# A two-block transformer forward pass: one factor per token for two norms in a row, and state-space decays by an fp32r product with a two-hot selector

## The chip, the cores and the metric

The kernel runs on one core of a Trainium2 chip. The metric is the device time of one execution in microseconds, lower is better. A core has TensorE (PE, products into PSUM), VectorE (DVE), ScalarE (ACT), GpSimd (POOL) and SyncE (SP, which issues DMA); each runs its own instructions in order, and they wait for each other on semaphores.

## The reference, cut to what matters

Two blocks run one after the other on 256 tokens of width 1024. The first has a hybrid mixer (a state-space mixer and gated linear attention), a cross-attention on 256 memory tokens and a SwiGLU feed-forward net, and ends with a norm. The second puts 16 meta tokens ahead, and has a stick-breaking attention, a squared-ReLU MLP, an RG-LRU mixer, a second MLP and a norm. The places that the change touches:

```python
def rmsnorm(x, g):                                 # rms_norm of the second block is the same
    return x * lax.rsqrt(jnp.mean(x * x, axis=-1, keepdims=True) + EPS) * g

# state-space mixer, per chunk of 64 tokens
a_cs = jnp.cumsum(a, axis=-1)                      # a = dt * A, 16 heads
Lmat = segsum_exp(a)                               # exp(a_cs[l] - a_cs[s]) for s <= l, else 0
y_diag = jnp.einsum('bcgls,bgrcls,bcsgrp->bclgrp', CB, Lmat, X)
...
# end of the first block, start of the second
h = h + swiglu(rmsnorm(h, norm_ffn[i]), w_ffn_in[i], w_ffn_out[i])
x = rmsnorm(h, norm_final)
...
h = jnp.concatenate([meta, x], axis=1)             # 16 + 256 tokens
hn = rms_norm(h, norm_mix[0])
h = h + stick_breaking_mixer(hn, sb_w_qkv[0], sb_w_o[0])
```

So the 256 real tokens pass two norms in a row at the border, with nothing between them; the 16 meta tokens pass the second alone.

## The kernel before

**Layout.** Activations lie transposed: feature on the 128 partitions, 8 blocks (KB) of features, tokens along the free dimension (T1 = 256, T2 = 272 with the meta tokens). The residual stream is hT. Weights come as a stream of 368 units of 128x1024 fp32 (`raw`, a ring of 4 buffers). For each unit ScalarE makes `whi`, the value rounded to fp32r (`split_hi`, L964), and VectorE makes `wlo`, the rest (`split_lo`, L1389). An operand is split likewise into `xh` (ScalarE, `operand`) and `xl` (VectorE, `operand_lo`, L1396). A product is then three fp32r products: xh·whi, xl·whi, xh·wlo (`products`, L420 to L422). A unit of TensorE is 8 feature blocks x 3 products into one of four `acc` banks, and `unit_done`, `lo_ready` and `evacuated` tie the engines together. The splits are made four units ahead.

**Norms.** The gain of a norm is multiplied into the operand before the product; the factor 1/rms of each token is applied to the product's result when VectorE moves it out of PSUM. The sum of squares comes from ScalarE's `square` of each block, VectorE's running sum over blocks (`add_stream_squares`, L1417), and an fp32 product with a matrix of 1/1024 (`stream_stats`, L481), which also spreads it over all partitions. `rms` (L982) takes the root on ScalarE, `inverse_rms` (L1430) the reciprocal on VectorE. For tokens on the partitions, products of one column give the same as columns (L485), and `rtok` holds the reciprocals.

**The border.** After the last of the 22 units of the FFN's second product (`ffo`), the statistics `fin1` are made, VectorE's `final` multiplies all eight blocks of hT by gain and factor (L1778), ScalarE and VectorE make xh, xl and squares of the result for the attention (norm `sb`), and TensorE's first unit of queries and keys waits for these block by block; the statistics `sb` follow behind that unit.

**The attention.** Queries and keys of a pair of heads (two units) alternate with scores and softmax-like terms of the pairs before (`sb_scores`, `soft_abs`, `soft_terms`, `soft_sum`, `soft_hi`, `soft_lo`, `sb_after`): the tiles sp, softp, softh, softl and wT. Then values (`token_pair`), scores of the last 16 queries (`tail_scores`) and the outputs.

**The decays.** `csn` holds the running sums of 16 heads on 16 partitions. `decay_row` of a head spreads its row over all 128 partitions: the stationary operand is one column of the identity, repeated 128 times, the product is in fp32 (L549), and two bf16 products (L550, L551) add a large number where the mask is zero. ScalarE takes the exponential, GpSimd multiplies with CB, and `ssd_out` reads the result two units later. Two rows come behind every second unit from the 28th to the 42nd.

The order of the work is written out by hand in each engine's program; no planner sets it.

## Time and profile before

| what | before |
|---|---|
| median of 3 runs | 1277.48 us (1276.99 to 1279.16) |
| profiled execution | 1278.51 us, span 1276.8 us |
| mean granted clock of TensorE | 0.985 |
| TensorE busy | 1218.4 us, 95% |
| VectorE, ScalarE, GpSimd busy | 67%, 52%, 3% |

A profile shows one execution. "Idle before" stands in square brackets behind an instruction with the engine and instruction that ended the idleness. An fp32 product is recorded as two instructions (x2), an fp32r product as one. Starts of matmuls are the better guide: their ends overlap the next one. The granted clock is a share of the full 2.4 GHz.

### The profile page before, as it was taken

The page shows a single profiled execution, that of the slowest core. Times are in us where ns is not written, and L with a number is a line of the kernel's source. Part 1 is how long each engine was busy: PE and PEld are TensorE (multiplying, and loading weights), DVE is VectorE, ACT ScalarE, POOL GpSimd, SP SyncE. Part 2 cuts the span into 40 slices and gives each one's busy share as a digit, 9 for nine tenths or more (in the row PEclk, how much of TensorE's full clock was granted, in tenths as well). Part 3 has the DMA queues.
Part 4 walks back from the last instruction along what each step waited for, and adds up shares of the span by engine and source line. Part 5 has one row for each costly group of instructions (what it writes and reads, how often), then busy time and mean ns, then how long its engine had stood idle before and what let it go on. Part 6 is the DMA issues. An engine that isn't in the chain of part 4 may idle for free.

```text
span 1276.8 us, 25597 instructions
## 1 busy us (share of the span) xinstructions
PE 1218.4 (95%) x9661; PEld 1179.2 (92%) x9661; DVE 860.8 (67%) x1295; ACT 666.1 (52%) x999; POOL 40.1 (3%) x59
## 2 busy tenths in 40 slices
PE   5989999999999999999799999999999888999996
PEld 5989879999999999999788899999999888999996
DVE  5897665798756777765676536666455969766443
ACT  6443435756534666654546325656344685666431
POOL 1001220200000000000100000000000000000000
PEclk9999999999999999999899999999999989999999
DMA  5455333466653566566433205555565435565661
GB/s 198 131 169 167 109 100 116 133 219 185 177 163 131 150 189 190 181 186 189 137 115 117 100 34 165 168 177 170 177 177 171 147 100 177 180 187 181 184 184 61
DMA packets 56761, 197.54 MB, mean 155 GB/s; under 512 B 7136, under 2 KB 9440, under 8 KB 56560
## 3 DMA queue, kind: packets, MB, share of 16 engines
q1 hardware_dynamic: 54144, 194.01, 49.4%
q10 hardware_dynamic: 2544, 2.51, 0.6%
q8 instruction: 52, 0.85, 0.3%
q14 instruction: 21, 0.17, 0.0%
HBM read 195.45 MB, written 1.05 MB: 154 GB/s over the span
## 4 chain that ended last, share of the span: by engine, by line
PE 80%; DVE 13%; ACT 4%; issue 2%; DMA 1%; SPq 0%; DVEq 0%; ACTq 0%
PE acc L420 22%; PE acc L422 22%; PE acc L421 22%; DVE wlo L1389 4%; PE acc L465 2%; PE acc L466 2%; PE acc L467 2%; ACT whi L964 2%; PE mix L549 1%; DVE xc L1593 1%; DVE uu L1921 1%; DMA raw<-w 1%; PE mix L711 1%; PE mix L692 1%; PE mix L791 1%
## 5 line engine op out<-in xcount | busy, mean ns | idle before, releaser
L964 ACT ACTIVATE whi<-raw 128x1024 fp32r<-128x1024 f32 x368 | 387.8, 1057 | 433.6 <-PE acc L422 373.8
L1389 DVE TENSOR_TENSOR wlo<-raw,whi 128x1024 fp32r<-128x1024 f32 x368 | 449.2, 1223 | 217.0 <-ACT whi L964 216.7
L420 PE MATMUL acc<-xh,whi 128*128 128x256 f32 (+1 forms) x1664 | 478.3, 287 | 25.0 <-DVE xl L1396 21.6
L421 PE MATMUL acc<-xl,whi 128*128 128x256 f32 (+1 forms) x1664 | 474.8, 285 | 0.0
L422 PE MATMUL acc<-xh,wlo 128*128 128x256 f32 (+1 forms) x1664 | 474.2, 285 | 0.0
L420 PEld LDWEIGHTS acc<-xh,whi 128*128 128x128 f32 x1664 | 317.2, 191 | 30.9 <-DVE wlo L1389 17.9
L422 PEld LDWEIGHTS acc<-xh,wlo 128*128 128x128 f32 x1664 | 317.6, 191 | 0.0
L421 PEld LDWEIGHTS acc<-xl,whi 128*128 128x128 f32 x1664 | 316.0, 190 | 0.2
L421 PE MATMUL acc<-hl,whi 128*128 128x256 f32 (+1 forms) x688 | 195.5, 284 | 0.0
L420 PE MATMUL acc<-hh,whi 128*128 128x256 f32 (+1 forms) x688 | 195.0, 283 | 0.0
L422 PE MATMUL acc<-hh,wlo 128*128 128x256 f32 (+1 forms) x688 | 194.7, 283 | 0.0
L422 PEld LDWEIGHTS acc<-hh,wlo 128*128 128x128 f32 x688 | 129.9, 189 | 0.0
L421 PEld LDWEIGHTS acc<-hl,whi 128*128 128x128 f32 x688 | 129.4, 188 | 0.0
L420 PEld LDWEIGHTS acc<-hh,whi 128*128 128x128 f32 x688 | 129.1, 188 | 0.0
L420 PE MATMUL acc<-yh,whi 128*128 128x256 f32 (+1 forms) x320 | 91.1, 285 | 6.8 <-DVE yl L1994 3.9
L422 PE MATMUL acc<-yh,wlo 128*128 128x256 f32 (+1 forms) x320 | 90.5, 283 | 0.0
L421 PE MATMUL acc<-yl,whi 128*128 128x256 f32 (+1 forms) x320 | 90.4, 283 | 0.0
L420 PEld LDWEIGHTS acc<-yh,whi 128*128 128x128 f32 x320 | 60.4, 189 | 8.2 <-DVE wlo L1389 5.1
L422 PEld LDWEIGHTS acc<-yh,wlo 128*128 128x128 f32 x320 | 60.5, 189 | 0.0
L421 PEld LDWEIGHTS acc<-yl,whi 128*128 128x128 f32 x320 | 60.1, 188 | 0.0
L465 PE MATMUL acc<-whi,xh 128*128 128x256 f32 (+1 forms) x160 | 47.0, 294 | 2.8 <-DVE wlo L1389 2.8
L1871 DVE SCALAR_TENSOR_TENSOR t<-acc,rstd 128x272 f32<-128x272 f32 (+1 forms) x64 | 27.7, 432 | 31.3 <-PE acc L422 30.9
(327 smaller groups left out, 1440.7 us busy)
## 6 DMA issues: line engine op xcount, KB each, us to landing
raw<-w SPq DMA_DIRECT2D x368, 512.0 KB, 3.6
hT<-xT ACTq DMA_DIRECT2D x1, 1024.0 KB, 10.5
mem<-memT ACTq DMA_DIRECT2D x1, 1024.0 KB, 5.8
out<-hT SPq DMA_DIRECT2D x8, 128.0 KB, 2.0
xdt<-wsmall ACTq DMA_DIRECT2D x1, 192.0 KB, 10.6
pr<-par ACTq DMA_DIRECT2D x1, 114.0 KB, 10.2
hT<-metaT ACTq DMA_DIRECT2D x1, 64.0 KB, 12.4
bcn<-wa ACTq DMA_DIRECT2D x1, 32.0 KB, 10.2
```

What stands on the lines that cost most here:

```text
L420: nc.tensor.matmul(dst, whi[:, slot, n, :], rh, start=first, stop=False)
L421: nc.tensor.matmul(dst, whi[:, slot, n, :], rl, start=False, stop=False)
L422: return nc.tensor.matmul(dst, wlo[:, slot, n, :], rh, start=False, stop=last)
L465: nc.tensor.matmul(dst, ah[:, k, at:at + n], whi[:, s:s + 2, k, :], start=k == 0, stop=False)
L466: nc.tensor.matmul(dst, ah[:, k, at:at + n], wlo[:, s:s + 2, k, :], start=False, stop=False)
L467: last = nc.tensor.matmul(dst, al[:, k, at:at + n], whi[:, s:s + 2, k, :], start=False, stop=k == KB - 1)
L549: nc.tensor.matmul(dst[:, 0:384], sel, csn[:, :], start=True, stop=False)
L692: last = nc.tensor.matmul(mix[:, h % 2, 256 * t:256 * t + 256], xqT[:, 2 * h + i, P * t:P * t + P], xkT[:, 2 * h + i, :], start=i == 0, st ...
L711: last = nc.tensor.matmul(mix[:, xbank[h], 256 * vb:256 * vb + 256], xv[:, mt, c:c + P], probT[:, h, mt, :], start=mt == 0, stop=mt == 1)
L964: act.activation(whi[:, j, :, :].rearrange("p k c -> p (k c)"), raw[:, j, :], ACT.Copy)\
L1389: dve.tensor_tensor(wlo[:, j, :, :].rearrange("p k c -> p (k c)"), raw[:, j, :], whi[:, j, :, :].rearrange("p k c -> p (k c)").bitcast(F32 ...
L1871: dve.scalar_tensor_tensor(out=t4[:, j, 0:T], in0=acc[:, j, 0:T], scalar=0.0, in1=rstd[:, 0:T], op0=ALU.max, op1=ALU.mult).then_inc(evacua ...
```

## The change

**The decays.** The running sums are stored in `cs2`, a tile of fp32r over 128 partitions that is zero except for two copies: rows 0 to 15 hold the rounded value, rows 32 to 47 the rest. The stationary operand `sel2` has a one at row h and at row 32 + h. One fp32r product then spreads high and low part together.

**The border.** The two norms are taken as one. With r1 the factor of the first norm and s the mean square of its unscaled output (hT times the gain of `fin1`), the factor of the real tokens is 1/sqrt(s + EPS * (mean square of hT + EPS)), and the gain is the product of both gains (`both`). So the operands of the attention come straight from hT. They are made during `ffo`, as each block of the FFN's output is finished, with their squares in a tile `sqb`. The meta tokens' part is made at the start of `ffo`. The first unit of queries starts behind `ffo`; then come two statistics products, of `sb` and of `fin1`, the latter in its own bank. The factors of tokens on partitions are made by products of one column out of `rstd` (`token_scales`). The stream itself still needs the first norm: its reciprocal and the multiplications of hT (`stream_rms`, `stream_normed`) now stand in the values part of the attention.

```diff
         "st_gla0", "st_gla1", "st_mem", "st_xattn", "pt0", "pt1", "pt2", "pt3",
-        "st_ffn", "st_fin1", "st_sb", "st_mlp0", "st_lru", "st_mlp1", "st_fin2"]
+        "st_ffn", "st_sb", "st_fin1", "tok_sb", "st_mlp0", "st_lru", "st_mlp1", "st_fin2"]
 R = {name: n for n, name in enumerate(MISC)}
...
+BANK["st_fin1"], FREE["st_fin1"] = 2, R["st_sb"]
 OPER = {name: n for n, name in enumerate(["mix", "xattn", "ffn", "sb", "mlp0", "lru", "mlp1"])}
-STAT = {name: n for n, name in enumerate(["mix", "xattn", "ffn", "fin1", "sb", "mlp0", "lru", "mlp1", "fin2"])}
-
-
-SUMS = {name: KB - 2 if name in ("fin1", "fin2") else KB - 1 for name in STAT}
+STAT = {name: n for n, name in enumerate(["mix", "xattn", "ffn", "fin1", "mlp0", "lru", "mlp1", "fin2"])}
+
+
+SUMS = {name: KB - 2 if name == "fin2" else KB - 1 for name in STAT}
 SUM0 = {name: sum(SUMS[x] for x in list(STAT)[:n]) for name, n in STAT.items()}
...
         csn = sb("csn", [16, 384], stack=s1)
+        cs2 = sb("cs2", [P, 384], F32R, stack=s1)
+        sel2 = sb("sel2", [P, SSD_HEADS], F32R, stack=s1)
         ctok = sb("ctok", [P, 4, 16], stack=s1)
...
             pool.memset(one16[0:16, :], 1.0).then_inc(consts, 1)
-            pool.wait_ge(consts, 9)
+            pool.memset(khk[:, 0, 0:384], 0.0).then_inc(consts, 1)
+            pool.wait_ge(consts, 10)
+            pool.tensor_copy(cs2[:, :], khk[:, 0, 0:384]).then_inc(consts, 1)
...
                 dst = mix[:, h % 2, :]
-                sel = ident[0:16, h:h + 1].broadcast_to([16, P])
-                nc.tensor.matmul(dst[:, 0:384], sel, csn[:, :], start=True, stop=False)
+                sel = sel2[:, h:h + 1].broadcast_to([P, P])
+                if h == 0:
+                    pe.wait_ge(sums_lo, 2)
+                nc.tensor.matmul(dst[:, 0:384], sel, cs2[:, :], start=True, stop=False)
                 nc.tensor.matmul(dst[:, 0:P], identb[:, :], bigm[:, :], start=False, stop=False)
...
-            stream_stats("fin1", T1)
             HB = SSD_HEADS + XH
                 for i in range(2):
+                    if m + i == 0:
+                        pe.wait_ge(metal_ready, 1)
                     unit("sqk", 2 * m + i, (2 * m + i) % 4, xh, xl, T2, ready=operand("sb") if m + i == 0 else None)
                     if m + i == 0:
-                        stream_stats("sb", T2, tiles2)
+                        pe.wait_ge(sumb_ready, KB)
+                        mean_squares("st_sb", [sqb[:, KB - 1, :]], T2)
+                        stream_stats("fin1", T1)
+                if m == 1:
+                    token_scales()
+
+            def token_scales():
+
+                dst = misc_bank("tok_sb")
+                pe.wait_ge(rstd_ready, 5)
+                for t, (at, n) in enumerate(tiles2):
+                    last = nc.tensor.matmul(dst[0:n, t:t + 1], rstd[:, at:at + n], ident[:, 0:1], start=t == 0, stop=True,
+                                            skip_group_check=True)
+                last.then_inc(misc_ready, 1)
...
                 if p == 1:
-                    pe.wait_ge(misc_free, R["st_sb"] + 1)
+                    pe.wait_ge(misc_free, R["tok_sb"] + 1)
                 if p >= 2:
...
                         act.activation(sg1[:, c % 4, :], xc[:, c, :], ACT.Tanh).then_inc(conv_th, 1)
+                    if m == 5:
+                        act.wait_ge(dt_step, 5)
+                        act.activation(cs2[0:16, :], csn[:, :], ACT.Copy).then_inc(sums_hi, 1)
                     if m == 6:
...
                 split_hi(u0 + n + 4)
+                if n == 0:
+                    act.wait_ge(unit_done, u0)
+                    act.wait_ge(meta_ready, 1)
+                    act.activation(xh[:, :, 0:META], mtok[:, :, :], ACT.Copy).then_inc(metah_ready, 1)
+                    act.wait_ge(meta_in, 16)
+                    act.activation(sqb[:, :, 0:META], hT[:, :, 0:META], ACT.Square).then_inc(metasq_ready, 1)
                 if (FFN_KB * m + FFN_KB - 1) // 8 == n:
                     act.wait_ge(evacuated[m % 4], (OUTS["ffo"] + m) // 4 + 1)
+                    h = hT[:, m, META:T2]
+                    act.activation(xh[:, m, META:T2], h, ACT.Copy, scale=both[:, m:m + 1]).then_inc(xh_ready, 1)
+                    act.activation(sqb[:, m, META:T2], h, ACT.Square, scale=g("fin1", m)).then_inc(sqb_ready, 1)
                     square(m, T1)
                     m += 1
-            rms("fin1", T1, (), 4)
-            act.wait_ge(meta_in, 16)
-            for b in range(KB):
-                act.wait_ge(fin_step, b + 1)
-                operand("sb", b, T2)
-            rms("sb", T2, (P, P, META), 5)
+            act.wait_ge(misc_ready, R["st_sb"] + 1)
+            act.wait_ge(rstd_ready, 4)
+            act.activation(rt[:, 0:META], mix[:, MISCB, 0:META], ACT.Sqrt, bias=EPS)
+            act.activation(rt[:, META:T2], mix[:, MISCB, META:T2], ACT.Sqrt, bias=EPS * EPS).then_inc(misc_free, 1)
+            act.wait_ge(misc_ready, R["st_fin1"] + 1)
+            act.activation(rtf[:, :], mix[:, BANK["st_fin1"], 0:T1], ACT.Sqrt, bias=EPS).then_inc(misc_free, 1)
...
                                                  op0=ALU.add, op1=ALU.mult).then_inc(conv_out, 1)
+                    if m == 17:
+
+                        dve.wait_ge(sums_hi, 1)
+                        dve.tensor_tensor(cs2[32:48, :], csn[:, :], cs2[0:16, :].bitcast(F32), ALU.subtract)\
+                            .then_inc(sums_lo, 1)
+                        dve.tensor_tensor(sel2[:, :], ident[:, 0:16], ident[:, 32:48], ALU.add).then_inc(sums_lo, 1)
                     if m == 22:
...
                 split_lo(u0 + n + 4)
+                if n == 0:
+                    f_, s_ = PC["fin1"], PC["sb"]
+                    dve.tensor_tensor(both[:, :], pr[:, f_:f_ + KB], pr[:, s_:s_ + KB], ALU.mult).then_inc(both_ready, 1)
+                    dve.wait_ge(meta_in, 16)
+                    dve.tensor_tensor(mtok[:, :, :], hT[:, :, 0:META], pr[:, s_:s_ + KB]
+                                      .rearrange("p (k o) -> p k o", o=1).broadcast_to([P, KB, META]), ALU.mult)\
+                        .then_inc(meta_ready, 1)
+                    dve.wait_ge(metah_ready, 1)
+                    dve.tensor_tensor(xl[:, :, 0:META], mtok[:, :, :], xh[:, :, 0:META].bitcast(F32), ALU.subtract)\
+                        .then_inc(metal_ready, 1)
                 if (FFN_KB * m - 1) // 8 == n:
-                    add_stream_squares("fin1", m - 1, T1)
+                    b = m - 1
+                    dve.wait_ge(xh_ready, KB * OPER["sb"] + b + 1)
+                    dve.scalar_tensor_tensor(out=xl[:, b, META:T2], in0=hT[:, b, META:T2], scalar=both[:, b:b + 1],
+                                             in1=xh[:, b, META:T2].bitcast(F32), op0=ALU.mult, op1=ALU.subtract)\
+                        .then_inc(xl_ready, 1)
+                    if b:
+                        if b == 1:
+                            dve.wait_ge(metasq_ready, 1)
+                        dve.wait_ge(sqb_ready, b + 1)
+                        if b > 1:
+                            dve.wait_ge(sumb_ready, b - 1)
+                        dve.tensor_tensor(sqb[:, b, :], sqb[:, b, :], sqb[:, b - 1, :], ALU.add).then_inc(sumb_ready, 1)
+                    add_stream_squares("fin1", b, T1)
+            dve.wait_ge(sumb_ready, KB - 1)
+            dve.wait_ge(sum_ready, SUM0["fin1"] + KB - 1)
+            dve.scalar_tensor_tensor(out=sqb[:, KB - 1, META:T2], in0=sq[:, KB - 1, 0:T1], scalar=EPS,
+                                     in1=sqb[:, KB - 1, META:T2], op0=ALU.mult, op1=ALU.add).then_inc(sumb_ready, 1)
                 inverse_rms(name, T)
-                for j in range(4):
-                    dve.wait_ge(evacuated[j], OUTS["sqk"] // 4)
                 for b in range(KB):
-            final("fin1", T1)
-            dve.wait_ge(fin_step, KB)
-            for b in range(KB):
-                operand_lo("sb", b, T2, KB * OPER["sb"] + b)
-                add_stream_squares("sb", b, T2)
-            inverse_rms("sb", T2, (P, P, META))
+            def stream_normed(first):
+
+                for b in range(first, first + 4):
+                    h = hT[:, b, META:T2]
+                    dve.scalar_tensor_tensor(out=h, in0=h, scalar=g("fin1", b), in1=rstdh[:, 0:T1], op0=ALU.mult,
+                                             op1=ALU.mult).then_inc(fin_step, 1)
+
+            def stream_rms():
+
+                dve.wait_ge(misc_free, R["st_fin1"] + 1)
+                dve.reciprocal(rstdh[:, 0:T1], rtf[:, :]).then_inc(rstd_ready, 1)
+                norms[0] += 1
+                dve.wait_ge(rstd_ready, norms[0])
+
+            def token_scales():
+
+                dve.wait_ge(misc_ready, R["tok_sb"] + 1)
+                dve.tensor_copy(rtok[:, 0:2], mix[:, MISCB, 0:2]).then_inc(tok_ready, 1)
+                dve.tensor_copy(rtok[0:META, 2:3], mix[0:META, MISCB, 2:3]).then_inc(misc_free, 1)
+
+            inverse_rms("sb", T2)
...
                 key_rows(2 * m + 1)
+                if m == 1:
+                    token_scales()
             for m in range(PAIRS, PAIRS + 3):
                 values(m - PAIRS)
+                if m == PAIRS:
+                    stream_rms()
+                else:
+                    stream_normed(4 * (m - PAIRS - 1))
```

The engines' orders at three places. Operands are out<-in by the program's names. VectorE at the end of `ffo`, before: residual sum (hT), weight split (wlo), then the factor, the stream and the operands.

```order
L1766 TENSOR_TENSOR hT<-acc,hT 128x256
L1389 TENSOR_TENSOR wlo<-raw,whi 128x1024
L1430 RECIPROCAL rstd<-rt 128x256
L1778 SCALAR_TENSOR_TENSOR hT<-hT,pr,rstd 128x256 x8
L1396 SCALAR_TENSOR_TENSOR xl<-hT,pr,xh 128x272 x2
L1417 TENSOR_TENSOR sq<-sq 128x272
```

And now:

```order
L1813 TENSOR_TENSOR hT<-acc,hT 128x256
L1430 TENSOR_TENSOR wlo<-raw,whi 128x1024
L1829 SCALAR_TENSOR_TENSOR xl<-hT,both,xh 128x256
L1838 TENSOR_TENSOR sqb<-sqb 128x272
L1458 TENSOR_TENSOR sq<-sq 128x256
L1842 SCALAR_TENSOR_TENSOR sqb<-sq,sqb 128x256
L1471 RECIPROCAL rstd<-rt 128x272
L1882 SCALAR_TENSOR_TENSOR sqd<-acc,rstd 64x272 x2
```

The operand xl of the last block and three sums of squares stand right behind the last weight split; the reciprocal and eight multiplications ahead of xl are gone, and so are the operands of the other seven blocks, which stand earlier.

TensorE at the end of the first unit of queries, before (sq,mean is the statistics, 128x1 the token columns):

```order
L422 MATMUL acc<-xh,wlo 128x272
L481 MATMUL mix<-sq,mean 128x272
L485 MATMUL mix<-mean,sq 128x1 x2
L485 MATMUL mix<-mean,sq 16x1
L420 MATMUL acc<-xh,whi 128x272
```

And now:

```order
L434 MATMUL acc<-xl,whi 128x272
L435 MATMUL acc<-xh,wlo 128x272
L494 MATMUL mix<-sqb,mean 128x272
L494 MATMUL mix<-sq,mean 128x256
L433 MATMUL acc<-xh,whi 128x272
```

The one-column products are gone from here; a second statistics product of 256 columns stands in their place, and the one ahead of the unit (`sq,mean 128x256 x2`) is gone.

VectorE in the values part, before (sv is a values tile):

```order
L1815 SCALAR_TENSOR_TENSOR softp<-mix,sp 128x768
L1820 TENSOR_TENSOR softl<-softp,softh 128x768
L1466 TENSOR_SCALAR sv<-acc,rtok 16x256
L1469 TENSOR_SCALAR sv<-acc,rtok 128x256 x2
L1389 TENSOR_TENSOR wlo<-raw,whi 128x1024 x2
L1809 TENSOR_SCALAR sp<-mix 128x768
```

And now:

```order
L1901 SCALAR_TENSOR_TENSOR softp<-mix,sp 128x768
L1906 TENSOR_TENSOR softl<-softp,softh 128x768
L1507 TENSOR_SCALAR sv<-acc,rtok 16x256
L1510 TENSOR_SCALAR sv<-acc,rtok 128x256 x2
L1430 TENSOR_TENSOR wlo<-raw,whi 128x1024 x2
L1862 RECIPROCAL rstdh<-rtf 128x256
L1895 TENSOR_SCALAR sp<-mix 128x768
```

A reciprocal stands between the weight splits and the next pair's sp.

## Rows read from the trace of the kernel before

**Rows 1.** The page's chain that ended last, its share by engine.

```profile
PE 80%; DVE 13%; ACT 4%; issue 2%; DMA 1%; SPq 0%; DVEq 0%; ACTq 0%
```

**Rows 2.** Waits of PE in 580 to 660 us: total, times, longest.

```profile
PE acc L420 <- DVE xl L1396: 6.3, 1, 6.3
...
PE mix L803 <- DVE softl L1820: 1.0, 1, 1.0
```

**Rows 3.** Windows, decay stretch: us, busy (count) per engine, PEclk, DMA, GB/s.

```profile
115.00:125.00 10.00, 10.00 (x66) 7.34 (x67) 7.82 (x10) 6.57 (x12) 3.69 (x3) 1.00 0.59 183
```

**Rows 4.** Timeline of PE, one decay row: start, us, instruction, idle before.

```profile
160.44 0.91 PE L549 MATMUL mix<-csn,ident 16*128 16x384 f32 x2
161.28 0.23 PE L550 MATMUL mix<-bigm,identb 128*128 128x128 bf16 x1
...
161.50 0.91 PE L549 MATMUL mix<-csn,ident 16*128 16x384 f32 x2
```

**Rows 5.** Timeline of PE, fp32r products in the attention loop.

```profile
668.77 0.39 PE L803 MATMUL mix<-softl,ntri 128*128 128x512 f32 x1
669.00 0.28 PE L805 MATMUL mix<-softl,nones 128*128 128x256 f32 x1
669.11 0.28 PE L811 MATMUL mix<-softl,ntri 128*128 128x256 f32 x1
```

**Rows 6.** Timelines of DVE and PE, end of the convolutions.

```profile
93.24 0.42 DVE L1598 SCALAR_TENSOR_TENSOR xc<-sg,xc 128x256 f32<-128x256 f32 x1
...
94.66 0.59 PE L530 MATMUL mix<-xc 128*128 128x256 f32 x2
95.09 0.38 PE L531 MATMUL mix<-xc 128*128 128x128 f32 x2
```

**Rows 7.** Timeline of PE over the border between the blocks.

```profile
624.05 0.27 PE L422 MATMUL acc<-hh,wlo 128*128 128x256 f32 x1
...
633.24 0.56 PE L420 MATMUL acc<-xh,whi 128*128 128x272 f32 x1 [6.25 <-DVE xl L1396]
...
638.63 0.62 PE L481 MATMUL mix<-sq,mean 128*128 128x272 f32 x2
639.09 0.63 PE L485 MATMUL mix<-mean,sq 128*128 128x1 f32 x6
639.65 0.39 PE L420 MATMUL acc<-xh,whi 128*128 128x272 f32 x1
```

**Rows 8.** Timeline of DVE over the border.

```profile
624.36 0.42 DVE L1766 TENSOR_TENSOR hT<-acc,hT 128x256 f32<-128x256 f32 x1 [0.40 <-PE acc L422]
625.51 1.22 DVE L1389 TENSOR_TENSOR wlo<-raw,whi 128x1024 fp32r<-128x1024 f32 x1 [0.73 <-ACT whi L964]
...
629.30 3.26 DVE L1778 SCALAR_TENSOR_TENSOR hT<-hT,pr,rstd 128x256 f32<-128x256 f32 x8
...
637.60 0.49 DVE L1396 SCALAR_TENSOR_TENSOR xl<-hT,pr,xh 128x272 fp32r<-128x272 f32 x1
638.01 0.43 DVE L1417 TENSOR_TENSOR sq<-sq 128x272 f32<-128x272 f32 x1
...
640.53 1.82 DVE L1430 RECIPROCAL rstd<-rt 128x272 f32<-128x272 f32 x1
```

**Rows 9.** Timeline of ACT over the border.

```profile
625.38 0.40 ACT L968 ACTIVATE sq<-hT 128x256 f32<-128x256 f32 x1
...
629.88 0.52 ACT L972 ACTIVATE xh<-hT,pr 128x272 fp32r<-128x272 f32 x1 [2.40 <-DVE hT L1778]
```

**Rows 10.** Timeline of DVE, first sp of the attention loop.

```profile
651.33 0.95 DVE L1809 TENSOR_SCALAR sp<-mix 128x768 uint32<-128x768 uint32 x1
```

**Rows 11.** Timeline of DVE, after the tail scores.

```profile
732.51 0.96 DVE L1809 TENSOR_SCALAR sp<-mix 128x768 uint32<-128x768 uint32 x1 [3.54 <-PE mix L794]
```

**Rows 12.** Windows, the clock: columns as in rows 3.

```profile
630.00:635.00 5.00, 1.76 (x8) 1.79 (x9) 4.96 (x14) 5.00 (x14) 0.05 (x1) 0.50 0.00 0
650.00:700.00 50.00, 47.39 (x330) 42.28 (x329) 33.54 (x43) 27.36 (x33) 0.00 (x0) 1.00 0.39 123
```

12 lines of the change are left out of this document (10 added, 2 removed).

## The prediction

> **What bounds the kernel now.** I read the page first, for which engine is the bound: TensorE carries 80% of the chain that ended last, VectorE only 13% [rows 1]. So time comes back in two ways only: less work in TensorE's queue, or a stretch in which TensorE stands still for another engine. The waits of TensorE over the border between the two blocks show the second kind: 6.3 us for xl, by far the largest wait there [rows 2]. Then I read three timelines: TensorE's in the state-space stretch (115 to 194 us), for what one row of decays costs; TensorE, VectorE and ScalarE between 624 and 650 us; and VectorE alone in two places where the change gives it more to do. In the state-space stretch the reader is to see that TensorE is never idle and VectorE is busy at most 7.8 of 10 us [rows 3], so a shorter TensorE instruction there is time gained.
>
> **Part 1, the decay rows.** One decay row is an fp32 product of 384 columns in two passes and two bf16 products of 128 columns. The row that starts at 160.44 us reaches its first bf16 product at 161.28 and the next row at 161.50: 0.84 + 0.22 = 1.06 us [rows 4]. The change keeps the 0.22 and makes the product one fp32r instruction. The trace has no fp32r product of 384 columns. The nearest rows: of 512 columns, 0.23 us from start to start (668.77 to 669.00), and of 256 columns 0.12 us (669.00 to 669.11) [rows 5]. I take the middle, 0.175 us. A row then costs 0.395 us, it saves 0.665 us, and 16 rows save 10.6 us. The ends are 9.8 us (0.23) and 11.4 us (0.12). If its weights were loaded in the open (about 0.19 us, the duration of a load in the same group's row), 7.6 us would be left.
> The Trainium skill, TensorE: Matmul & The Clock Gate, "Back-to-back issue gap", gives columns / 2.4 + 2.5 ns for one product and, for a stream of weight loads and products, about 131 ns at 512 columns. This trace has 0.23 us for 512 columns in such a stream, so it bears out the first formula (216 ns) and not the second. By the first, 384 columns would take an estimated 0.163 us and part 1 would save 10.8 us; by the second it would save over 11.2 us.
>
> What part 1 adds: on ScalarE one copy of 16x384; on GpSimd a memset and a copy in the first microseconds, long before TensorE asks for the constants; on VectorE a subtraction of 16x384 and a tiny sum, some 0.6 us together (a product of 256 elements per partition takes 0.42 [rows 6]). These two stand in unit 17, in a stretch where VectorE is the bound. The next thing due behind them is the last convolution, which ends at 93.24 + 0.42 = 93.66 us; the product that reads it starts at 94.66 [rows 6]. So 1.0 us of cover for 0.6 us: I cost it at nothing, and at 0.6 us if the cover is gone. In the decay stretch two rows come in each pair of units, so 10 us of before become about 8.7, and VectorE's 7.8 of 10 [rows 3] becomes 7.8 of 8.7: it still fits.
>
> **Part 2, the border.** Before: the last product of the FFN starts at 624.05. But for the statistics, TensorE does nothing until 633.24, when the first xl of the next block arrives; that unit ends at 638.63, its statistics at 639.65, where the second unit starts [rows 7]. From the last product's end (624.17, one issue of 0.12 later) to the second unit are 15.5 us, of which a unit at full rate is 24 products x 0.126 = 3.0 us.
> After: eight operands of the new block are made from hT while the FFN still runs, with the product of both gains, so only block 7 is late. Its path, in durations of before's rows:
> VectorE adds the residual at 624.36 and is then held by its weight split, which waits for ScalarE's and runs from 625.51 to 626.65 [rows 8]. ScalarE has finished its weight split by 625.4, where its next instruction starts, then xh (0.4), the scaled square (0.4) and the plain square (0.4), until 626.5 [rows 9]. VectorE's xl of block 7 then runs 626.65 to 627.13 (0.49 [rows 8]). TensorE has by then done the 21 products of blocks 0 to 6 (624.17 + 2.64 = 626.81) and waits 0.4 us; the unit ends at 627.6. Three more VectorE sums (0.4 each [rows 8], the last after its own predecessor's end) bring the last summand at 628.35, so TensorE waits 0.8 us more. Two statistics products of 272 and 256 columns at 0.46 and 0.43 (638.63 to 639.09 is one) end at 629.25, and the second unit starts there instead of at 639.65: 10.4 us gained.
> Behind that, ScalarE has two roots, a table load and the weight split in front of unit 4, as before; VectorE's reciprocal of 1.82 us [rows 8] starts some 0.4 us after the statistics' end instead of 0.9 us. Nothing here comes later against the second unit than it did.
> The three token factors are now one-column products behind the fourth unit (some 0.5 us; before, six such passes took 639.09 to 639.65 and their time is in the 15.5). In the attention loop that follows, the chain runs over VectorE and ScalarE, and TensorE waits 1.0 us for the first softl [rows 2], so these products are covered. Not covered are VectorE's two copies of the factors (0.3 us), which stand ahead of the first sp at 651.33 [rows 10]. Net: 10.1 us, with ends of 8.0 (the clock falls, below) and 11.0 (the summand earlier).
>
> What part 2 puts elsewhere: in the FFN's second product VectorE gets 0.85 us and ScalarE 0.8 us more in every output of 7.8 us of TensorE, and both stood idle there for longer than that; the splits are made three units ahead. The final norm of the first block goes into the end of the attention: a reciprocal of about 1.76 us behind the first values, and twice four products of 0.41 (eight took 3.26 [rows 8]) behind the second and the third. The sp at 732.51 was released by TensorE's tail scores after 3.54 us of idleness of VectorE [rows 11], so the first four (1.65 us) fit ahead of it, and the softl that the reciprocal delays is read only behind those scores. The last four stand ahead of yl, which the output projection wants only after another values product. I cost all of it at nothing; without cover it would be 1.76 + 3.26 = 5.0 us.
>
> **Sum.** 10.6 + 10.1 = 20.7 us. The profiled execution took 1278.51 us (span 1276.8), the median of the runs is 1277.48; the same saving from the median gives 1256.8 us.
>
> **The rivals.**
> *The clock falls at the border.* Before, TensorE's granted clock was 0.50 in 630 to 635 us, that is 1.2 of 2.4 GHz, after 6 us of idleness [rows 12], and the first 15 products of the unit came 0.227 us apart and not 0.126: 1.5 us, all returned in my sum. After, two waits of 0.4 and 0.8 us stand within 2.5 us. If they bring the same fall, 2 us are lost: 1258.8. Against: the waits of up to 1.0 us in the attention loop [rows 2] left the clock at 1.00 there [rows 12]. The Trainium skill, TensorE: Matmul & The Clock Gate, "What's actually happening", says that activity releases the throttle and idleness brings it back; by it the fall of before goes with its idle stretch, and the trace agrees.
> *The decay stretch becomes VectorE's.* It would then give back less: if half the 10.6 us turns into waits for wlo, or for the GpSimd product ahead of each output, 1262.1. For it: VectorE at 7.8 of 10. Against: four units of lead, and that the products read in a row's unit were made a pair of units before.
> *The product isn't one pass* (the change doesn't do what it says). Two fp32 passes over all 128 rows took 0.43 us for 256 columns (94.66 to 95.09 [rows 6]); for 384 that would be 0.65 us, part 1 saves 3.0 us, and the time is 1264.4. Against: every fp32r instruction of before is one record, every fp32 one two [rows 4, 5].
> *Slower.* The mechanism would be the half clock over the whole decay stretch: the short fp32r products leave TensorE's work there in small pieces. The stretch holds some 68 us of TensorE work after the change; each us at half clock costs up to 1, so it has to hold for over 21 us to eat the gain, and over all 68 it gives up to 1325. Against: its clock is 1.00 [rows 3], with the same small bf16 products in it, and the work that goes is the slow part.
>
> **How the numbers follow.** My forecast 0.74, the clock 0.10, VectorE in the decay stretch 0.07, not one pass 0.04, slower 0.02, and 0.03 for savings larger than my ends. A difference under 0.2%, 2.6 us, can't be told from none here. Only the slower case and a strong form of the others reach it: faster 0.96, same 0.02, slower 0.02. The own terms reach from 9.8 + 8.0 to 11.4 + 11.0, that is 1255.1 to 1259.7; the weights in the open give 1259.8; with VectorE's case and a rest of scatter of 1 us the range is 1253.8 to 1262.5.
>
> **What would show it.** The product of the decay row as 16 records, 0.40 us from one row to the next; TensorE still without waits from 115 us on. At the border, TensorE idle for about 1.2 us in two waits (xl, then the last sum), clock 1.00, the second unit 5 us after the FFN's end. The first softl's wait as before or longer by 0.3 us, and none added past 700 us. The forecast is wrong if the decay rows stay above 0.6 us, if waits for wlo appear among them, or if the first unit of the second block starts cold.

## The result, and the profile after

| what | before | after |
|---|---|---|
| median (5 runs each) | 1277.48 us (1276.18 to 1279.16) | 1256.92 us (1256.07 to 1258.57) |
| profiled execution | 1278.51 us, span 1276.8 | 1256.76 us, span 1255.0 |
| mean granted clock of TensorE | 0.985 | 0.987 |
| VectorE, ScalarE busy in the span | 67%, 52% | 68%, 53% |

The ratio is 0.9837 with a 95% interval of [0.9826, 0.9848]: faster by 20.6 us in the medians, 21.8 us in the two spans. The forecast was 1256.8 us. Of all the executions in this document one, of norm_early (experiment 8), took 1668.08 us at a mean granted clock of 0.655; it stands in no comparison.

TensorE's share of the chain that ended last fell by one point, as VectorE's rose [rows 1]. Page of the changed kernel, its chain that ended last, by engine:

```profile
PE 79%; DVE 14%; ACT 4%; issue 2%; DMA 1%; SPq 0%; DVEq 0%; ACTq 0%
```

**Where the time came from.** I laid the TensorE instructions of the two traces side by side and took, for each pair of the same instruction, the start after minus the start before:

| place (time in the trace before) | after minus before, us |
|---|---|
| first unit, 13 us | -0.3 |
| first instruction that reads the last convolution, 94.66 us | -0.3 |
| behind the last of the 16 decay rows, about 185 us | -11.7 |
| first unit of the second block, 633 us | -20.7 |
| its second unit, 639.65 us | -22.1 |
| 10 us further | -21.4 |
| 20 us further | -21.9 |
| end of the span | -21.8 |

So all of it comes from two places, 11.5 us from the decay rows and 10.2 us from the border. Between them and behind them the curve is flat to some tenths: nothing was given back in the FFN, and nothing in the attention. (At 43 us the clock fell at different moments in the two traces and at 88 us in one alone; the curve leaves its level there by 0.7 and 1.3 us, and comes back each time.)

**The decay rows after.** Timeline of TensorE in the changed kernel, one pair of rows: start, us, instruction.

```profile
161.43 0.28 PE L435 MATMUL acc<-xh,wlo 128*128 128x256 f32 x1
161.54 0.34 PE L564 MATMUL mix<-cs,sel 128*128 128x384 f32 x1
161.72 0.23 PE L565 MATMUL mix<-bigm,identb 128*128 128x128 bf16 x1
161.79 0.22 PE L566 MATMUL mix<-bigm,identb 128*128 128x128 bf16 x1
161.82 0.42 PE L564 MATMUL mix<-cs,sel 128*128 128x384 f32 x1
162.08 0.23 PE L565 MATMUL mix<-bigm,identb 128*128 128x128 bf16 x1
162.15 0.22 PE L566 MATMUL mix<-bigm,identb 128*128 128x128 bf16 x1
162.30 0.66 PE L577 MATMUL mix<-sq,xdt 128*64 128x256 f32 x4
```

The product is one record, and its first bf16 product follows 0.18 us after it, against 0.84 before [rows 4]. From one row's first bf16 product to the next row's there are 0.36 us (161.72 to 162.08); before it was 1.06. From the unit's last product to the first instruction behind the pair of rows it takes 0.87 us (161.43 to 162.30). The same two ends in the trace before:

```profile
160.23 0.28 PE L422 MATMUL acc<-xh,wlo 128*128 128x256 f32 x1
...
162.55 0.44 PE L562 MATMUL mix<-sq,xdt 128*64 128x256 f32 x2
```

That is 2.32 us. 2.32 - 0.87 = 1.45 us per pair, and 8 pairs make 11.6 us. Windows of the changed kernel over the decay stretch and over the border: us, busy (count) of TensorE, weight loads, VectorE, ScalarE and GpSimd, granted clock, DMA share, GB/s.

```profile
114.00:124.00 10.00, 10.00 (x87) 9.20 (x86) 8.60 (x11) 6.80 (x13) 3.58 (x2) 1.00 0.65 188
612.00:622.00 10.00, 9.19 (x68) 8.62 (x67) 7.34 (x11) 7.59 (x11) 5.57 (x4) 1.00 0.40 118
```

TensorE is still never idle among the decay rows, and VectorE went from 7.8 to 8.6 of 10 us [rows 3]: closer to its limit, and not over it.

**The border after.** Timeline of TensorE in the changed kernel; the first line is the last product of the FFN.

```profile
612.37 0.28 PE L435 MATMUL acc<-hh,wlo 128*128 128x256 f32 x1
612.48 0.29 PE L433 MATMUL acc<-xh,whi 128*128 128x272 f32 x1
...
615.52 0.39 PE L433 MATMUL acc<-xh,whi 128*128 128x272 f32 x1 [0.23 <-DVE xl L1829]
...
616.74 0.73 PE L494 MATMUL mix<-sqb,mean 128*128 128x272 f32 x2 [0.59 <-DVE sqb L1842]
617.30 0.59 PE L494 MATMUL mix<-sq,mean 128*128 128x256 f32 x2
617.55 0.48 PE L433 MATMUL acc<-xh,whi 128*128 128x272 f32 x1
```

Where TensorE stood for 6.25 us for xl [rows 7], the first unit now follows the FFN at once; two waits of 0.23 and 0.59 us are left, and the second unit starts 5.07 us behind the start of the first (617.55 - 612.48). Waits of TensorE in the changed kernel, 570 to 660 us, all of them (total, times, longest):

```profile
PE mix L832 <- DVE softl L1906: 1.2, 3, 0.4
PE mix L494 <- DVE sqb L1842: 0.6, 1, 0.6
PE acc L433 <- DVE xl L1829: 0.2, 1, 0.2
```

The 6.3 us for xl are gone [rows 2], and the first softl is waited for 0.4 instead of 1.0 us: the token products stand in that gap. (Over the same instructions of the trace before, the three waits for softl came to 1.8 us; now they come to 1.2.)

VectorE over the border in the changed kernel:

```profile
612.68 0.42 DVE L1813 TENSOR_TENSOR hT<-acc,hT 128x256 f32<-128x256 f32 x1 [0.41 <-PE acc L435]
613.84 1.23 DVE L1430 TENSOR_TENSOR wlo<-raw,whi 128x1024 fp32r<-128x1024 f32 x1 [0.73 <-ACT whi L993]
614.98 0.48 DVE L1829 SCALAR_TENSOR_TENSOR xl<-hT,both,xh 128x256 fp32r<-128x256 f32 x1
615.38 0.43 DVE L1838 TENSOR_TENSOR sqb<-sqb 128x272 f32<-128x272 f32 x1
615.73 0.42 DVE L1458 TENSOR_TENSOR sq<-sq 128x256 f32<-128x256 f32 x1
616.26 0.43 DVE L1842 SCALAR_TENSOR_TENSOR sqb<-sq,sqb 128x256 f32<-128x256 f32 x1
```

This is the order that the prediction walked through: residual, the weights' remainder that waits for ScalarE, xl, three sums. What stands between TensorE and the second unit is now this queue, and in it the weights' remainder of 1.23 us, which nobody needs at once.

**One wait is new**, and it is not one that the forecast had. Waits of TensorE over the whole changed kernel, the line in question:

```profile
PE mix L543 <- DVE xc L1639: 1.1, 1, 1.1
```

It cost nothing against before (the curve is at -0.3 there), because TensorE came to that place 1.3 us earlier. The experiments below take it apart.

### The profile page after: what moved, and what is told of

Same layout as the page of the kernel before. It is cut to its first block, busy times and chain, and to the rows that moved or that the text cites. A ratio compares the mean times of both kernels' runs of the same rounds, so it can differ in the third digit from the quotient of the medians.

```text
span 1255.0 us, 25571 instructions
## 1 busy us (share of the span) xinstructions
PE 1204.0 (96%) x9643; PEld 1173.8 (94%) x9643; DVE 858.5 (68%) x1301; ACT 666.8 (53%) x1000; POOL 42.9 (3%) x61
## 4 chain that ended last, share of the span: by engine, by line
PE 79%; DVE 14%; ACT 4%; issue 2%; DMA 1%; SPq 0%; DVEq 0%; ACTq 0%
PE acc L433 22%; PE acc L435 22%; PE acc L434 22%; DVE wlo L1430 5%; PE acc L478 2%; PE acc L479 2%; PE acc L480 2%; ACT whi L993 2%; DVE xc L1634 1%; DVE uu L2013 1%; DMA raw<-w 1%; PE mix L726 1%; PE mix L707 1%; DVE sq L1458 1%; PE mix L820 1%
## 6 DMA issues: line engine op xcount, KB each, us to landing
xdt<-wsmall ACTq DMA_DIRECT2D x1, 192.0 KB, 10.6
pr<-par ACTq DMA_DIRECT2D x1, 114.0 KB, 10.4
bcn<-wa ACTq DMA_DIRECT2D x1, 32.0 KB, 10.4
```

## The experiments

Ten kernels ran. Differences of a few tenths of a us are read from the traces (start of the same TensorE instruction in both), since the medians scatter by about 1 us. "Before" on the same chip was 1279.02 us in the first four, 1278.56 in the next four, 1278.63 in the last two.

### 1 and 2. Each part alone

decay_only keeps the changed decay rows and puts the border of before back; border_only does the reverse. Their cores:

```diff
 (decay_only, against before)
-                sel = ident[0:16, h:h + 1].broadcast_to([16, P])
-                nc.tensor.matmul(dst[:, 0:384], sel, csn[:, :], start=True, stop=False)
+                sel = sel2[:, h:h + 1].broadcast_to([P, P])
+                nc.tensor.matmul(dst[:, 0:384], sel, cs2[:, :], start=True, stop=False)
...
 (border_only, against after)
-                sel = sel2[:, h:h + 1].broadcast_to([P, P])
-                nc.tensor.matmul(dst[:, 0:384], sel, cs2[:, :], start=True, stop=False)
+                sel = ident[0:16, h:h + 1].broadcast_to([16, P])
+                nc.tensor.matmul(dst[:, 0:384], sel, csn[:, :], start=True, stop=False)
...
-                    if m == 17:
```

> The decays' fp32r product alone, the border as before. Theory (the two parts are independent, and the first is worth what the aligned starts of TensorE showed between the two traces, 11.6 us over the 16 rows): 1277.5 - 11.6 = 1265.9 us, TensorE's starts ahead by 11.6 us between the first and the last decay row and by no more behind them. As forecast before the result: 10.6 us, 1266.9. Rival (part of the gain was only the profiled execution's, or hangs on the border too): less than 10 us, above 1267.5.

> The two norms as one at the border alone, the decays as before. Theory: 10.1 us saved, 1267.4 us; the second unit of queries starts 5.2 us after the FFN's last product instead of 15.6, and TensorE has no wait of 1.1 us for the convolutions at 94 us, since the two VectorE instructions of unit 17 are gone. Rival (the border's gain is given back in the attention loop, which runs over VectorE and ScalarE): under 8 us, above 1269.5.

Measured: decay_only 1266.81 us, ratio 0.9902 [0.9882, 0.9922]; border_only 1266.74 us, ratio 0.9907 [0.9888, 0.9925]. By the traces the decay rows alone bring 11.5 us (from -0.15 at the last convolution to -11.6 behind the last row) and the border alone 10.4 us to its second unit, 10.2 us net. The parts add up and do not touch each other: 11.5 + 10.2 = 21.7 us, against 21.8 in the spans of before and after. The medians do not show this: they save 12.2 and 12.3 us, 24.5 together, where both parts at once saved 20.6. In the profiled execution of border_only the surplus lies ahead of the border: it was 2.45 us ahead of before when it came there, 1.5 us of it from 43 us, where TensorE's clock fell in before and not in this one, and 0.9 us from the last convolution (below).

### 3. The product in fp32

```diff
-        cs2 = sb("cs2", [P, 384], F32R, stack=s1)
-        sel2 = sb("sel2", [P, SSD_HEADS], F32R, stack=s1)
+        cs2 = sb("cs2", [P, 384], stack=s1)
+        sel2 = sb("sel2", [P, SSD_HEADS], stack=s1)
```

> As the changed kernel, but cs2 and sel2 in fp32: the product of a decay row runs over all 128 rows in fp32, two passes. It tells one pass from full rows. Theory (columns and passes set it): 384 columns in two passes at the 0.43 us per 256 columns of full-row fp32 products are 0.65 us, a row some 0.75 us instead of 0.33, so 16 rows cost 6.8 us more: 1263.7 us. Rival A (the 16-row operand made the old product slow, not its two passes): near the changed kernel, 1257 to 1259. Rival B (only the passes count, rows give nothing): a row at 1.05 us as before, 11.6 us more, 1268.5.

Measured: 1264.14 us, ratio 0.9882 [0.9864, 0.9899]. Timeline of TensorE in decay_fp32, one pair of rows:

```profile
157.67 0.28 PE L435 MATMUL acc<-xh,wlo 128*128 128x256 f32 x1
157.79 0.81 PE L564 MATMUL mix<-cs,sel 128*128 128x384 f32 x2
158.43 0.22 PE L565 MATMUL mix<-bigm,identb 128*128 128x128 bf16 x1
...
159.45 0.66 PE L577 MATMUL mix<-sq,xdt 128*64 128x256 f32 x4
```

In fp32 the product is two records (x2) and takes 0.64 us to the first bf16 product, against 0.18 in fp32r. Between the same two ends a pair takes 1.78 us (157.67 to 159.45) instead of 0.87: 0.91 x 8 = 7.3 us. So the kind of the operands carries 7.3 of the 11.6 us. But 4.3 us are there without it (2.32 - 1.78 = 0.54 per pair): the two fp32 records over 128 partitions are 0.20 us shorter than the two over 16 (0.84 [rows 4]), and the way into each row is shorter too. My sum did not keep the two shares apart; the rival "not one pass" did, and had 3.0 us for this one.

### 4. Fewer partitions

The product over the 48 partitions that hold numbers, with the zeros of the other 80 left out; the sum is the same.

```diff
-                sel = sel2[:, h:h + 1].broadcast_to([P, P])
-                nc.tensor.matmul(dst[:, 0:384], sel, cs2[:, :], start=True, stop=False)
+                sel = sel2[0:48, h:h + 1].broadcast_to([48, P])
+                nc.tensor.matmul(dst[:, 0:384], sel, cs2[0:48, :], start=True, stop=False)
```

> As the changed kernel, but the fp32r product contracts over 48 partitions only (rows 0 to 47 hold all that is not zero). Theory (with fewer than all rows, the weights of the next product are loaded in the open, which is why an old row took 0.1 us longer per pass than its columns): a row 0.1 to 0.25 us longer, 1.6 to 4 us in all, 1258.5 to 1261. Rival (rows don't matter): the same as the changed kernel, 1256.9, and 0.65 us per pair of rows.

Measured: 1260.6 us (1259.24 to 1261.82), ratio 0.9861 [0.9843, 0.9878]. Less work takes longer, and the timelines show why. TensorE's products in decay_48:

```profile
173.24 0.28 PE L435 MATMUL acc<-xh,wlo 128*128 128x256 f32 x1
173.44 0.44 PE L564 MATMUL mix<-cs,sel 48*128 48x384 f32 x1
173.82 0.23 PE L565 MATMUL mix<-bigm,identb 128*128 128x128 bf16 x1
173.88 0.22 PE L566 MATMUL mix<-bigm,identb 128*128 128x128 bf16 x1
174.03 0.44 PE L564 MATMUL mix<-cs,sel 48*128 48x384 f32 x1
...
174.62 0.66 PE L577 MATMUL mix<-sq,xdt 128*64 128x256 f32 x4
```

The pair takes 1.38 us (173.24 to 174.62) against 0.87: 0.51 x 8 = 4.1 us.

Its weight loads there:

```profile
173.44 0.18 PEld L564 LDWEIGHTS mix<-cs,sel 48*128 48x128 f32 x1
173.81 0.10 PEld L565 LDWEIGHTS mix<-bigm,identb 128*128 128x128 bf16 x1 [0.19 <-issue]
...
174.03 0.18 PEld L564 LDWEIGHTS mix<-cs,sel 48*128 48x128 f32 x1
```

The weight loads of the changed kernel at the rows shown above:

```profile
161.31 0.19 PEld L435 LDWEIGHTS acc<-xh,wlo 128*128 128x128 f32 x1
161.43 0.19 PEld L564 LDWEIGHTS mix<-cs,sel 128*128 128x128 f32 x1
...
161.79 0.19 PEld L564 LDWEIGHTS mix<-cs,sel 128*128 128x128 f32 x1
```

With 128 partitions the load runs beside the product in front of it: it starts at 161.43 together with the last product of the unit, and the row's product starts 0.11 us later. With 48 the load and its own product carry the same start, 173.44, 0.20 us behind the last product; the first bf16 product comes 0.38 us later instead of 0.18, and the next row 0.15 us behind the last bf16 product instead of 0.03. So the load ahead of this product isn't hidden. The kernel before, with 16 partitions, has the same signs: 0.15 us between the last bf16 product and the next row [rows 4].

It isn't the small number of partitions by itself, though. The second fp32 record of a row stands behind one of the same 16 partitions. Its load and itself in the trace before:

```profile
160.55 0.18 PEld L549 LDWEIGHTS mix<-csn,ident 16*128 16x128 f32 x1
```

```profile
160.87 0.48 PE L549 MATMUL mix<-csn,ident 16*128 16x384 f32 x1
```

This load starts 0.32 us ahead of its product. And the bf16 product behind the row has all 128 partitions, yet at 161.28 its load starts only with it; over 128 partitions, in decay_fp32, the same load starts 0.32 us ahead (158.11 for 158.43). The rest of the traces say the same. In the changed kernel, 16 products stand behind one with another number of partitions (128 to 16 or 64, or back), and each has its load at most 0.003 us ahead of it; of the 28 with 16 or 64 partitions behind one with the same number, the 25 of 256 columns have it 0.21 us ahead. In decay_48 all 48 changes of the number have it at most 0.005 us ahead. So what puts the load in the open is the change of the number from one product to the next, and the row's product over 16 or 48 partitions makes two such changes, one into it and one out of it. That 128 partitions help is due to their neighbours having 128. This is read off the traces; no kernel was run for it.

### 5 and 6. The queue of VectorE at the last convolution

late_rest moves the two instructions of unit 17 to unit 19, behind the last convolution; more_17 adds two idle ones to them.

```diff
 (late_rest)
-                    if m == 17:
+                    if m == 19:
...
 (more_17, behind the two of unit 17)
+                        for q_ in range(2):
+                            dve.tensor_tensor(sq[0:16, q_, 0:272], csn[:, 0:272],
+                                              csn[:, 0:272], ALU.subtract)
```

> The changed kernel with one block moved: the remainder of the running sums and the two-hot matrix are formed behind the second convolution unit after unit 17 (at unit 19) and no longer at unit 17, ahead of the last convolution. Theory: the two instructions of 0.3 us each stand in VectorE's queue ahead of the convolution that TensorE waits for, and their cover had run out; then TensorE's wait for xc at 94 us falls from 1.1 to 0.4 to 0.6 us and everything behind comes 0.5 to 0.7 us earlier, 1256.3 us. Rival: VectorE was late for another reason (TensorE itself came 1.4 us earlier because its clock did not fall at 88 us), and the wait stays near 1.1 us. A difference of 0.6 us is below what the times can tell; the trace decides.

> The changed kernel with two more idle VectorE instructions (subtractions over 16 rows of 272 columns, into a buffer that nothing reads then) behind the two at unit 17. Theory: no cover is left there, so each adds its own duration (about 0.3 us) to TensorE's wait for xc at 94 us, which grows from 1.1 to about 1.7 us, and the time by 0.6 us to 1257.5 us. Rival: VectorE still has slack there and the wait stays at 1.1 us. The trace decides, not the times.

Measured: late_rest 1257.79 us, ratio 0.9841 [0.9826, 0.9857]; more_17 1257.44 us, ratio 0.9842 [0.9826, 0.9858]. Neither can be told from the changed kernel. The expectation for more_17 (a wait of 1.7 us) failed: it waits less than the changed kernel, 0.3 us:

```profile
PE mix L543 <- DVE xc L1639: 0.3, 1, 0.3
```

and late_rest doesn't wait at all. What decides is in the windows 84 to 94 us (columns as above). The kernel before:

```profile
84.00:94.00 10.00, 7.25 (x50) 7.05 (x50) 9.47 (x19) 2.73 (x4) 0.00 (x0) 0.83 0.53 175
```

The changed kernel:

```profile
84.00:94.00 10.00, 6.59 (x54) 6.18 (x52) 9.76 (x21) 3.32 (x5) 0.00 (x0) 1.00 0.48 143
```

late_rest:

```profile
84.00:94.00 10.00, 7.28 (x51) 7.08 (x50) 9.79 (x20) 2.73 (x4) 0.00 (x0) 0.83 0.56 164
```

more_17:

```profile
84.00:94.00 10.00, 7.28 (x49) 7.07 (x48) 9.76 (x22) 2.73 (x4) 0.00 (x0) 0.83 0.41 132
```

In the changed kernel's profile TensorE kept the full clock behind its idleness of 2.7 us at 85 us; in the three others it ran part of the next unit at half clock, 1.2 of 2.4 GHz. The same kernel run again (10, below) fell to 0.83 too, so this does not come with the change. Measured from the start of that unit (the first product behind the 2.7 us), with VectorE's last convolution:

| kernel | VectorE work ahead of it | convolution ends | TensorE reads it | wait | clock 84:94 |
|---|---|---|---|---|---|
| before | none | +6.11 us | +7.11 us | none | 0.83 |
| late_rest | none | +6.11 | +7.07 | none | 0.83 |
| border_only | none | +6.11 | +6.25 | 0.33 us | 1.00 |
| after | two | +6.89 | +7.03 | 1.1 | 1.00 |
| after, run again | two | +6.89 | +7.06 | none | 0.83 |
| more_17 | four | +7.59 | +7.73 | 0.3 | 0.83 |

The third column tells VectorE's part: two instructions move the end of the convolution by 0.78 us, two more by another 0.70 us, their whole length, since VectorE has no idle time in this stretch. TensorE is ready at +5.9 us at full clock (7.03 less the wait of 1.1) and at +7.1 to +7.3 if the clock fell. The six other profiles fit: decay_only, decay_fp32 and decay_48 kept the clock, and with the two instructions ahead they read at +7.04 after a wait of 1.1 us; last_first, norm_early and both_moves lost it and read at +7.3 without a wait. So the cover of 1.0 us that I read off before [rows 6] was made by the half clock. The two instructions are free only in executions with the fall, and cost 0.8 us in the others (+7.03 against border_only's +6.25). That half of the theory for late_rest (the instructions delay the convolution by their own length) is shown by the convolution's end; that the move shortens the run by 0.8 us at full clock was not seen, since neither execution profiled with the move kept the clock.

### 7. The queue of VectorE at the border

last_first: the weight preparation of the last unit of the FFN's output moves, on ScalarE and on VectorE, behind block 7's operand, squares and sums.

```diff
-                split_lo(u0 + n + 4)
+                if n < 21:
+                    split_lo(u0 + n + 4)
...
                                      in1=sqb[:, KB - 1, META:T2], op0=ALU.mult, op1=ALU.add).then_inc(sumb_ready, 1)
+            split_lo(u0 + 25)
```

> The changed kernel with the preparation of the weights for the fourth unit ahead (ScalarE's rounded part and VectorE's remainder, 1.2 us on VectorE) moved, for the last unit of the output projection alone, behind block 7's operand, squares and sums. Theory: what is left of the border is the queue of VectorE, where the weights' remainder stands ahead of the operand of block 7; the waits for xl (0.23 us) and for the last sum (0.59 us) go, the statistics end about 1.1 us earlier and nothing behind holds the gain up: 1255.8 us. Rival: the gain at the border's first unit is given back behind it, where the weights for the fourth unit come later or in TensorE's wait for the normed scores, and the time stays at 1256.9 us.

Measured: 1255.6 us (1254.56 to 1258.0), ratio 0.9828 [0.9812, 0.9844]. Timeline of TensorE in last_first:

```profile
614.73 0.68 PE L494 MATMUL mix<-sqb,mean 128*128 128x272 f32 x2
```

The statistics stand without a wait ahead of them, and so does the last block's product: both waits are gone. Against the changed kernel TensorE moves from -0.77 us (the offset that this execution had ahead of the border) to -2.01 at the statistics and -2.06 at the second unit: 1.3 us, and the curve is at -2.05 still at 700 us (-1.9 at the end). The rival, that it is given back, is out.

### 8. The first norm without its place

norm_early: the reciprocal and the eight multiplications of the stream move from the values part of the attention to the border.

```diff
+            stream_rms()
+            stream_normed(0)
+            stream_normed(4)
...
-                if m == PAIRS:
-                    stream_rms()
-                else:
-                    stream_normed(4 * (m - PAIRS - 1))
```

> The changed kernel with the root, reciprocal and eight multiplications of the stream's first norm (5.0 us on VectorE) moved from the part of the attention where the values are computed to directly behind the reciprocal of the border's statistics. Theory: at the border VectorE's queue feeds TensorE, which has only some 2 us of VectorE's idle time there as cover; about 3 us of the 5 come out on TensorE: 1260.0 us (1258.5 to 1262). Rival one: none is covered, 1261.9 us. Rival two: TensorE has enough queued work of its own, and the time stays at 1256.9 us.

Measured: 1259.95 to 1263.96 us, median 1261.2 us, ratio 0.9874 [0.9857, 0.989]. The profiled execution had 1259.95 us, span 1258.2, that is 3.2 us over the changed kernel. Timeline of VectorE in norm_early:

```profile
618.20 1.85 DVE L1471 RECIPROCAL rstd<-rt 128x272 f32<-128x272 f32 x1 [1.31 <-ACT rt L1239]
620.09 1.75 DVE L1862 RECIPROCAL rstdh<-rtf 128x256 f32<-128x256 f32 x1
621.87 3.26 DVE L1856 SCALAR_TENSOR_TENSOR hT<-hT,pr,rstdh 128x256 f32<-128x256 f32 x8
```

Its TensorE behind the first scores:

```profile
640.23 0.50 PE L832 MATMUL mix<-softh,ntri 128*128 128x512 f32 x1 [3.04 <-DVE softl L1909]
```

The 5.0 us of VectorE work reach TensorE 20 us later, as a wait of 3.04 us for the first softl where the changed kernel waits 0.4: 2.6 us in that wait, and 2.9 us from ahead of the border to behind it (+0.20 to +3.10 on the curve), the forecast of 3 us. So the place in the values part is worth about 3 us by the trace. The medians differ by 4.3 us from the changed kernel's, and by 3.4 to 3.8 us from those of late_rest and more_17, which ran on the same chip; whether the rest is scatter stays open.

### 9 and 10. Both moves, and the changed kernel again

both_moves joins late_rest and last_first; after_again is the changed kernel without an edit, on the same chip.

> The changed kernel with both moves at once: the remainder of the running sums and the two-hot matrix at unit 19 instead of 17, and the last weight preparation of the output projection behind block 7's operand, squares and sums. Theory: the moves are independent; the second is worth 1.0 to 1.2 us in every execution, the first 0.8 us in executions in which the clock of TensorE does not fall at 88 us and nothing in the others (there TensorE comes late enough by itself). Expected 1255.4 us, 1.1 to 1.9 us under the changed kernel on the same chip. Rival: the second unit's gain of last_first was a good execution, and the two kernels stand within 0.3 us of each other.

> The changed kernel once more, on the same chip as both_moves, as what that run is compared with, and for how far two executions of one kernel lie apart: 1256.9 us expected. In the trace the stretches at 34 to 54 us and at 88 to 91 us may show another granted clock than in its first profile, and if the clock falls at 88 us the wait for xc of 1.1 us at 94 us is gone.

Measured: both_moves 1255.61 us (1254.26 to 1257.7), ratio 0.9821 [0.9807, 0.9834]; after_again 1256.93 us (1256.63 to 1257.61), ratio 0.983 [0.9816, 0.9843]. The trace shows the border's 1.3 us once more (from -0.44 to -1.72 us between the two), and nothing from the other move, as its clock fell at 88 us in both. The medians are 1.3 us apart with intervals that overlap: shown by two traces, not by the times. By its ratio it can't be told from last_first (0.9828) either.

## Why the prediction was right

**The bound.** Right: time came back only where TensorE's queue became shorter (the decay rows) and where it had stood still (the border).

**Part 1** was forecast at 10.6 us and brought 11.6. The product itself is as taken, 0.18 us for 0.175, and from row to row I had 0.395 us where the trace has 0.36 to 0.38. What the sum left out is the way into a pair: the 0.21 us between the unit's last product and the first row's product (160.23 to 160.44) became 0.11 (161.43 to 161.54), since behind a product of 128 partitions the load of one over 128 runs beside it, and that of one over 16 does not. That is 0.10 us per pair, and 0.03 more inside it: 8 x 0.13 = 1.0 us. The term that was mis-sized is "a row then costs 0.395 us, it saves 0.665 us": 0.72 us per row, measured. Experiment 4 shows the mechanism. My lower bound of 7.6 us, "its weights loaded in the open", turns out to describe the 48-partition kernel: 11.6 - 4.1 = 7.5 us saved. That it fits to 0.1 us is luck: the open loads cost 4.1 us and not 3.0, and the base was 1.0 us low. The first formula of the Trainium skill (TensorE: Matmul & The Clock Gate, "Back-to-back issue gap") gave an estimated 0.163 us for 384 columns; the trace has 0.18, so columns / 2.4 is a floor that these fp32r products don't quite reach.

**The rival "not one pass"** is out by the record itself (x1), and experiment 3 gives its price: 7.3 us, for which I had 7.6 (1264.4 forecast, 1264.14 measured). It came out right although its base was 1 us off.

**VectorE at unit 17, "1.0 us of cover for 0.6 us".** This step failed. The cover was TensorE's half clock in the execution that I had read, and the price is 0.78 us. It did no harm to the total, because in the profile after, the same full clock that took the cover away had brought 1.3 us. Rows 6 alone could not show this; the window's clock of 0.83 from 84 to 94 us could have.

**Part 2** was forecast at 10.4 us to the second unit and brought 10.4 us (22.1 - 11.7). By the curve, 9.1 us of it came up to the start of the first unit (7.8 us of idleness, and the statistics that stood in it) and 1.9 us inside that unit; 0.5 us were lost again behind it, to the wait for the last sum and the second statistics product.

The 1.9 us inside the unit are not the clock's, to which I had put down 1.5 us. TensorE at the end of that unit, before:

```profile
637.38 0.39 PE L420 MATMUL acc<-xh,whi 128*128 128x272 f32 x1
...
638.15 0.39 PE L420 MATMUL acc<-xh,whi 128*128 128x272 f32 x1
```

At half clock three products of a block took 0.68 us, and VectorE made an xl every 0.77 us (637.60 is the last [rows 8]). Back at full clock TensorE had caught up and stood for xl twice; the last xl ended at 638.09 and its product started at 638.15. So VectorE's queue of xl set the end of that unit, and by these rows a full clock would have been spent waiting for it (not run). What the change gave back there is that queue. The sum isn't touched, as it goes from end to end.

From the FFN's end to the second unit I had 629.25 - 624.17 = 5.08 us and the trace has 5.07. The two waits were forecast at 0.4 and 0.8 us between starts. Between starts they are 0.4 us (615.52, where 21 products end at 615.13) and 0.7 us (616.74, where the unit ends at 616.00); the view's 0.23 and 0.59 count from modelled ends. The statistics began 0.08 us later than forecast and took 0.08 us less. Net of the attention loop, 10.1 forecast, 10.2 measured: the token products behind the fourth unit cost 0.7 us, and the shorter wait for softl gave 0.5 back. The rival of the clock is out: it was 1.00 over the border.

**What I had costed at nothing.** The FFN's additions: the curve is flat across it. The first norm in the values part: flat behind it, and experiment 8 shows that the same 5.0 us are not free elsewhere. The decay stretch as VectorE's: 8.6 of 10 us and no wait. (The splits in the FFN are made four units ahead, not three as that paragraph has it; nothing hung on it.)

**The total** is nearer than its parts: +1.0 us from part 1 and +0.1 from part 2 make 21.8 us against a forecast of 20.7, and the medians gave 20.6. A distance of 0.1 us between medians that each scatter by 1 us says nothing; the curve does. Not taken apart are the two halves of the border's change, the early operands and the one factor for two norms: I tried neither alone.

## What to carry to other kernels

Where weights change with every product and the neighbours use all 128 partitions, an operand filled up with zeros to 128 can be cheaper on TensorE than the few rows that matter; look whether the load's start lies ahead of its own product's. Before a wait is called cover for new work, read the granted clock around it: cover made by a half clock is there in one execution and gone in the next. When a border between stages is bound by another engine's queue, ask of each instruction in it who needs it and when: preparation for four units ahead does not belong in front of the operand that is awaited.

## What the hardware showed unexpectedly

- A weight load was not overlapped where the number of partitions changed from one product to the next: 0.38 us instead of 0.18 us for the same 384 columns at 48 partitions between products of 128, and 0.51 us per pair of rows in all. Behind a product of the same number, 16, 64 or 128, it was. Changes between 128 and 16, 48 or 64 were seen, no others.
- An fp32 record is slower than an fp32r one of the same shape: 0.32 us each at 128 partitions and 384 columns (0.64 for the two of a product), against 0.18. Whether one record is one pass isn't shown.
- The clock's falls behind one and the same idleness differ. Behind 2.7 us of waiting at 85 us, TensorE's clock fell in the profiles of before, late_rest, more_17, last_first, norm_early, both_moves and after_again, and did not in those of after, border_only, decay_only, decay_fp32 and decay_48. It moves what stands there by 1.3 to 1.5 us. The four kernels measured on one chip (decay_only to decay_48) all kept the clock and the six on two others all lost it; what decides it isn't shown.
